# Moving the per-layer embedding's products behind the first experts, in a one-core decoder step

## The reference, cut to what matters

```
x = x + mixed @ w_o                                   # 520 rows of 1024
h2 = rmsnorm(x, g_ffn)
group: top 1 of 4; experts in it: top 2 of 8          # router, 36 logits per row
x = x + sum over the 2 chosen e of gate_e * (silu(h2 @ w_gate[e]) * (h2 @ w_up[e])) @ w_down[e]
gate = sigmoid(rmsnorm(x, g_ple) @ w_ple_gate)
x = x + (p @ w_ple) * gate                            # p: 520 rows of 256, an input
y = rmsnorm(x, g_final)
```

## Time and profile before

| | us |
|---|---|
| median of 3 runs | 1034.40 |
| the profiled execution | 1035.33 |
| its span in the trace | 1033.5 |
| TensorE busy | 867.0 (84%) |
| VectorE busy | 348.3 (34%) |
| ScalarE busy | 196.0 (19%) |
| GpSimd busy | 261.2 (25%) |
| DMA | 316.42 MB, mean 306 GB/s |
| chain that ended last | TensorE 53%, DMA 35% (the up weights 31%) |

### The profile page before, as it was taken

The page is one execution under the profiler, slowest core; times in us unless marked ns, Lnnn a source line. Parts: engine busy times, 40 slices in busy tenths (PEclk is TensorE's granted clock), DMA queues, the critical chain, the costliest instruction groups (busy, mean ns, idle before and its releaser), DMA issues.

```text
span 1033.5 us, 11650 instructions
## 1 busy us (share of the span) xinstructions
PE 867.0 (84%) x4281; PEld 450.8 (44%) x4281; DVE 348.3 (34%) x710; ACT 196.0 (19%) x393; POOL 261.2 (25%) x342
## 2 busy tenths in 40 slices
PE   5999888988969988899877878798877869783994
PEld 3888565755633545434332333233333323331442
DVE  5899966545424565213000000000000000011652
ACT  3110234423420121212101010101101011010431
POOL 6989775222210000202111110101111010001110
PEclk9999978998979996989998898988999898997998
DMA  9899954378994225269999999999999999997111
GB/s 308 325 337 381 326 211 164 133 280 346 361 370 166 101 103 212 73 256 414 404 408 400 408 403 407 413 395 412 410 408 420 394 410 403 428 408 295 74 42 41
DMA packets 53831, 316.42 MB, mean 306 GB/s; under 512 B 11246, under 2 KB 24110, under 8 KB 33048
## 3 DMA queue, kind: packets, MB, share of 16 engines
q1 hardware_dynamic: 34736, 233.28, 56.6%
q0 software_dynamic: 14480, 76.17, 19.4%
q10 hardware_dynamic: 4576, 6.46, 1.8%
HBM read 309.31 MB, written 14.82 MB: 314 GB/s over the span
## 4 chain that ended last, share of the span: by engine, by line
PE 53%; DMA 35%; DVE 5%; issue 2%; ACT 2%; POOL 2%; SPq 1%; POOLq 0%; DVEq 0%; ACTq 0%
DMA arena<-in_w_up 31%; PE psum L1692 14%; PE psum L1277 8%; PE psum L1359 7%; PE psum L1805 5%; PE psum L1507 5%; PE psum L1422 2%; PE psum L1644 2%; DMA arena<-in_w_down 1%; PE psum L1371 1%; DMA arena<-in_cache_v,indices 1%; PE psum L1401 1%; PE psum L1707 1%; PE psum L1530 1%; PE psum L1383 1%
## 5 line engine op out<-in xcount | busy, mean ns | idle before, releaser
L1692 PE MATMUL psum<-arena 128*64 128x512 f32 x1024 | 270.8, 689 | 82.3 <-DMA arena<-in_w_up 82.3
L1692 PEld LDWEIGHTS psum<-arena 128*64 128x64 f32 x1024 | 91.8, 158 | 237.3 <-issue 235.5
L2405 DVE TENSOR_TENSOR arena<-arena,psum 64x512 f32<-64x512 f32 x32 | 22.1, 691 | 376.2 <-ACT arena L1132 376.2
L1707 PE MATMUL psum<-arena 128*64 128x512 f32 x512 | 116.0, 592 | 3.6 <-DMA arena<-in_w_down 3.6
L1277 PE MATMUL psum<-arena 128*128 128x260 f32 x384 | 86.8, 388 | 0.1
L789 POOL COPY indices<-row_list 128x1 int32 (+1 forms) x26 | 4.6, 177 | 308.6 <-ACT arena L1138 308.6
L1359 PE MATMUL psum<-arena 128*128 128x260 f32 x320 | 80.1, 404 | 2.4 <-DVEq L1969 2.4
L1132 ACT ACTIVATE arena<-psum 64x512 f32<-64x512 f32 x32 | 18.9, 589 | 332.2 <-PE psum L1692 332.2
L720 POOL TENSOR_TENSOR arena<-arena 128x2048 f32<-128x2048 f32 x18 | 81.5, 4533 | 1.0 <-DMA arena<-in_cache_k,indices 0.7
L1277 PEld LDWEIGHTS psum<-arena 128*128 128x128 f32 x384 | 73.8, 193 | 12.8 <-issue 1.2
L1877 DVE TENSOR_REDUCE arena<-arena 128x32 f32<-128x2048 f32 x32 | 72.0, 2281 | 4.6 <-POOL arena L720 3.5
(11 more groups left out here) (331 smaller groups left out, 878.6 us busy)
## 6 DMA issues: line engine op xcount, KB each, us to landing
arena<-in_w_down SPq DMA_DIRECT2D x32, 2048.0 KB, 25.3
arena<-in_w_gate SPq DMA_DIRECT2D x31, 2048.0 KB, 18.4
arena<-in_w_up SPq DMA_DIRECT2D x31, 2048.0 KB, 22.9
arena<-in_w_in SPq DMA_DIRECT2D x11, 1024.0 KB, 7.6
arena<-in_x_prompt SPq DMA_DIRECT2D x8, 512.0 KB, 7.8
arena<-in_w_ple_gate SPq DMA_DIRECT2D x1, 4096.0 KB, 26.2
arena<-moe_rows SPq DMA_DIRECT2D x4, 1024.0 KB, 7.9
out<-arena ACTq DMA_DIRECT2D x8, 256.0 KB, 4.6
```

What stands on the lines that cost most here:

```text
L1692: last = mm(bank(s)[m * SLOTS:(m + 1) * SLOTS, :], hgT[s][:, k, :], w_gu[s][m][:, k, :], start=(k == 0), stop=(k == DC - 1))
L1707: last = mm(bank(6 + s)[n * SLOTS:(n + 1) * SLOTS, :], actT[s][:, k, :], w_dn[s][:, k, n * BANK:(n + 1) * BANK], start=(k == 0), stop=(k = ...
```

## The change

- The transposes of p (now transpose_p_tiles, three groups: tiles 0 and 4, tiles 1 and 2, tile 3) stand behind the experts 1, 2 and 3, and embed(0) to embed(4) behind the experts 4 to 8. They use banks 2 and 3, and wait for the counts and overflow lists that use the same banks.
- LEAD goes from RING + 1 = 5 to 2 * RING + 1 = 9: nine experts are written out on TensorE, VectorE and ScalarE, GpSimd's part likewise, and the loops begin a turn later.
- p's loads are issued by ScalarE behind the last stores of h2 instead of long before, to another place in SBUF; pT has one buffer per tile.
- The fills p01, p23 and p4 are gone, so the fills behind them change banks.
- On ScalarE copy_h2T(2) stands ahead of store_h2(QT). On VectorE second_norm(3) stands ahead of take_logits(QT).

```diff
-LEAD = RING + 1
+LEAD = 2 * RING + 1
+FIRST_LOOP = LEAD // RING
+P_MOVES = ((0, 4), (1, 2), (3,))
+EMBED_FROM = 1 + len(P_MOVES)
...
-         + ["rank1", "rank2"] + [f"h{QT}{s}" for s in "abr"] + ["p01", "p23", "p4"] + [f"h3{s}" for s in "abr"] + ["rank4", "rank3"])
+         + ["rank1", "rank2"] + [f"h{QT}{s}" for s in "abr"] + [f"h3{s}" for s in "abr"] + ["rank4", "rank3"])
...
-        pT = at(c4 + 2 * D, 2, NT)
-        p_nat = at(c4 + 2 * D + 2 * NT, TILES, DP)
+        p_nat = at(region_c + 3 * D, TILES, DP)
+        pT = [at(region_c + 3 * D + t * DP, 2, P) for t in range(TILES)]
...
 # ScalarE
             second_norm(QT)
+            copy_h2T(2)
             store_h2(QT)
-            copy_h2T(2)
             second_norm(3)
             copy_h2T(QT)
-            for name, t0, n in (("p01", 0, 2), ("p23", 2, 2), ("p4", 4, 1)):
-                wait_full(act, name)
...
             store_h2(3)
             copy_h2T(3)
...
-            copy_p_emb(0)
-            copy_p_emb(1)
             act.wait_ge(h2_stored[0], 48)
             act.wait_ge(h2_stored[1], 32)
-            for t in range(2, TILES):
-                copy_p_emb(t)
+            act.dma_start(p_nat[:, 0:QT, :], a["p_prompt"][0, 0].rearrange("(t p) n -> p t n", p=P)).then_inc(ple_in, 16)
+            act.dma_start(p_nat[0:NB, QT, :], a["p_sample"][0].rearrange("b l n -> (b l) n")).then_inc(ple_in, 16)
...
+                if 1 <= e < EMBED_FROM:
+                    copy_pT_tiles(e - 1)
+                if e >= EMBED_FROM:
+                    copy_p_emb(e - EMBED_FROM)
-            with act.Fori(1, NE // RING - 1) as i:
+            with act.Fori(FIRST_LOOP, NE // RING - 1) as i:
...
 # TensorE
             route(QT)
-
-            pe.wait_ge(ple_in, 48)
-            pes = (("p01", (0, 1)), ("p23", (2, 3)), ("p4", (4,)))
...
             transpose_h2(3)
-            embed(0)
             route_logits(3)
-            embed(1)
             rank_rows(QT)
             for t in (0, 1, 2):
                 list_rows(t)
-            embed(2)
             rank_rows(3)
             list_rows(QT)
             list_rows(3)
-            embed(3)
-            embed(4)
-
-            pe.wait_ge(pe_free, TILES)
...
+            def transpose_p_tiles(g):
+                if g == 0:
+                    pe.wait_ge(ple_in, 48)
+                if g == 1:
+                    pe.wait_ge(route_op, ROUTE_AT["over"])
+                if g == 2:
+                    pe.wait_ge(pe_free, 2)
+                for n, t in enumerate(P_MOVES[g]):
+                    w = tile_width(t)
+                    for k in range(2):
+                        first = n * 2 * P + k * P
+                        last = tr(bank(3 if g else 2)[:, first:first + w], p_nat[0:w, t, k * P:(k + 1) * P], ident[0:w, 0:w])
+                last.then_inc(pe_full, 1)
+
+            def embed(t):
+
+                w = tile_width(t)
+                pe.wait_ge(pe_free, len(P_MOVES) + t)
+                if t == 0:
+                    pe.wait_ge(lists_ready, 3)
+                for n in range(2):
+                    for k in range(2):
+                        last = mm(bank(2 + n)[0:w, :], pT[t][:, k, 0:w], w_ple_sb[:, k, n * BANK:(n + 1) * BANK],
+                                  start=(k == 0), stop=(k == 1))
+                last.then_inc(pe_full, 1)
...
             def list_over():
                 pe.wait_ge(route_op, ROUTE_AT["over"])
+                pe.wait_ge(pe_free, 1)
...
+                if 1 <= e < EMBED_FROM:
+                    transpose_p_tiles(e - 1)
+                if e >= EMBED_FROM:
+                    embed(e - EMBED_FROM)
-            with pe.Fori(1, NE // RING - 1) as i:
+            with pe.Fori(FIRST_LOOP, NE // RING - 1) as i:
...
 # VectorE
             place_rows(2)
+            second_norm(3)
             take_logits(QT)
-            second_norm(3)
             top_two(QT)
```

More of the change, by code:

```diff
@@ L192, in build @@
         assert c4 + 6 * D <= c3 + PAGE * HC
-        pT = at(c4 + 2 * D, 2, NT)
-        p_nat = at(c4 + 2 * D + 2 * NT, TILES, DP)
+        p_nat = at(region_c + 3 * D, TILES, DP)
+        pT = [at(region_c + 3 * D + t * DP, 2, P) for t in range(TILES)]
+        assert TILES * DP <= 2 * D
         w_gu = [[at(r + m * DC * BANK, DC, DE) for m in range(2)] for r in (region_b, region_a)]
@@ L375, in build @@
         lists_ready, list_full = sem("lists_ready"), sem("list_full")
-        ple_in, pe_full, pe_free = sem("ple_in"), sem("p_emb_full"), sem("p_emb_copied")
+        ple_in, pe_full, pe_free = sem("ple_in"), sem("p_full"), sem("p_copied")
         y_out = [sem(f"y_out{s}") for s in range(RING)]
@@ L812, in _ @@
             pool.wait_ge(lists_ready, 2)
-            for c in range(RING):
+            for c in range(FIRST_LOOP * RING):
                 move_rows(0, c)
             base = step.n
-            with pool.Fori(1, NE // RING - 1) as i:
-                step.off = (i - 1) * (2 * RING)
+            with pool.Fori(FIRST_LOOP, NE // RING - 1) as i:
+                step.off = (i - FIRST_LOOP) * (2 * RING)
                 for c in range(RING):
                     move_rows(i, c)
-            step.n, step.off = base + 2 * RING * (NE // RING - 2), 0
+            step.n, step.off = base + 2 * RING * (NE // RING - 1 - FIRST_LOOP), 0
             for e in range(NE - RING, NE + 2):
@@ L1044, in _ @@
             stored[0] += 4
-            act.wait_ge(rms_ready, 1)
-            act.dma_start(p_nat[:, 0:QT, :], a["p_prompt"][0, 0].rearrange("(t p) n -> p t n", p=P)).then_inc(ple_in, 16)
-            act.dma_start(p_nat[0:NB, QT, :], a["p_sample"][0].rearrange("b l n -> (b l) n")).then_inc(ple_in, 16)
             def second_norm(t):
@@ L1091, in _, with copy_pT_tiles @@
             second_norm(QT)
+            copy_h2T(2)
             store_h2(QT)
-            copy_h2T(2)
             second_norm(3)
             copy_h2T(QT)
-            for name, t0, n in (("p01", 0, 2), ("p23", 2, 2), ("p4", 4, 1)):
-                wait_full(act, name)
-                w = n * P if n == 2 else NB
-                act.activation(pT[:, :, t0 * P:t0 * P + w], fill(name).rearrange("p (k n) -> p k n", k=2)[:, :, 0:w],
-                               ACT.Copy).then_inc(free_of(name), 1)
             store_h2(3)
             copy_h2T(3)
+            act.wait_ge(h2_stored[0], 48)
+            act.wait_ge(h2_stored[1], 32)
+            act.dma_start(p_nat[:, 0:QT, :], a["p_prompt"][0, 0].rearrange("(t p) n -> p t n", p=P)).then_inc(ple_in, 16)
+            act.dma_start(p_nat[0:NB, QT, :], a["p_sample"][0].rearrange("b l n -> (b l) n")).then_inc(ple_in, 16)
+            def copy_pT_tiles(g):
+                act.wait_ge(pe_full, g + 1)
+                for n, t in enumerate(P_MOVES[g]):
+                    w = tile_width(t)
+                    src = bank(3 if g else 2)[:, n * 2 * P:(n + 1) * 2 * P].rearrange("p (k n) -> p k n", k=2)
+                    ins = act.activation(pT[t][:, :, 0:w], src[:, :, 0:w], ACT.Copy)
+                ins.then_inc(pe_free, 1)
             def copy_p_emb(t):
                 w = tile_width(t)
-                act.wait_ge(pe_full, t + 1)
-                pair = psum[0:w, 2 * (t % 2):2 * (t % 2) + 2, :]
-                act.activation(p_emb[0:w, t, :].rearrange("p (a n) -> p a n", a=2), pair, ACT.Copy).then_inc(pe_free, 1)
-            copy_p_emb(0)
-            copy_p_emb(1)
-            act.wait_ge(h2_stored[0], 48)
-            act.wait_ge(h2_stored[1], 32)
-            for t in range(2, TILES):
-                copy_p_emb(t)
+                act.wait_ge(pe_full, len(P_MOVES) + t + 1)
+                act.activation(p_emb[0:w, t, :].rearrange("p (a n) -> p a n", a=2), psum[0:w, 2:4, :], ACT.Copy).then_inc(pe_free, 1)
             def route_exps():
@@ L2416, in _ @@
                     overflow_lists()
-            with dve.Fori(1, NE // RING - 1) as i:
+            with dve.Fori(FIRST_LOOP, NE // RING - 1) as i:
                 for q in range(RING):
```

## The result

The kernel after took 1020.95 us, the median of 4 runs (1019.79 to 1022.33), against 1035.16 us for the kernel before (median of 4 runs, one more than the three behind 1034.40); the ratio is 0.9878, with a 95% interval of 0.9833 to 0.9922. Run again beside the experiments it gave 0.9908 (0.9878 to 0.9938) and 0.9855 (0.9830 to 0.9879). So the change makes the kernel 10 to 15 us faster. The forecast was 1019.3, a gain of 15.

What follows compares the result with a forecast made beforehand. The experts' weight stream bounds the kernel, its end set by expert 0's products. Savings 5.4 + 3.9 + 2.65 + 3.5 = 15.45 us take the profiled 1035.33 to 1019.9 and the median to 1018.95; forecast 1019.3, range 1015.5 to 1024.5.

Steps and rivals of the forecast that it cites:

- What bounds the kernel: Experts' weight stream, DMA busy from 447 to 930 us: the end follows when expert 0's gate and up products end.
- X: The date when SyncE issues expert 2's weights, at 446.30 us in the kernel before; the label comes from the experiments.
- Part A: Tile 2's copies ahead of the samples' store, up to T: 5.4 us earlier, 1.87 from waiting and 3.5 from clock.
- T: End of the last output projection half of tile 3, forecast to move from 398.71 to 393.35 us.
- Rival 1: TensorE's clock falls all the same at Part A's short gap, or another wait replaces it: price 3.5 us, time 1022.8, chance 0.15.
- Part B: T to R, with tile 3's norm first and p's work gone: 12.3 us in place of 16.2, 3.9 less.
- R: End of tile 3's router logits on TensorE, at 414.94 us in the kernel before.
- Part C: R to G, tile 3's placing no longer waiting for TensorE in embed(2): 8.4 us in place of 11.05, 2.65 less.
- G: Start of GpSimd's first gather, at 425.99 us in the kernel before.
- Part D: G to expert 0's products, without embed(3) and embed(4): 7.1 us in place of 10.6, 3.5 less.
- What is put behind: p's ten transposes and five embeds on TensorE behind experts 1 to 8: cost 0, covered by the weight queue's reserve.

Runs made afterwards that it cites:

- late_start: The kernel after with 16 idle TensorE products of 512 columns ahead of expert 0's gate and up products; 1032.14 us, ratio 0.9982 to the kernel before.
- no_swaps: The kernel after with both order swaps undone (tile 2's copies on ScalarE, tile 3's norm on VectorE), only p moved; 1024.80 us, ratio 0.9920 to before.
- no_embed: The kernel after without the five embeds' products, p_emb filled by ScalarE from a row of w_ple instead; 1021.26 us, ratio 0.9879 to before.
- double_embed: The kernel after with each embed's products issued twice, the second overwriting the first with the same values; 1023.57 us, ratio 0.9899 to before.
- lead_only: The kernel before with nine experts written out instead of five and loops from turn 2, nothing else; 1033.65 us, ratio 0.9999 to before.

## Why the prediction was right

Of the forecast 15.45 us, counted from the start of tile 2's transposes, the first profile after has 14.1 (64.13 to 50.04) and the two others 15.9 and 16.2.

- **What bounds the kernel**: right. X to the end is 587.2 before and after; with 14.3 us put ahead of X (late_start) it is 587.6.
- **Part A, up to T**: forecast 5.4, and the one part that came out otherwise in the recorded profile. The waiting was right: TensorE's gap is 0.89 us, forecast 0.95. The clock was right in five of eight profiles, which save 5.3, and wrong in three, the recorded one among them, which saves 3.6. Rival 1 (chance 0.15) named the cause, but at half its price: 1.7 us, not 3.5, because the clock stayed low about half as long (387.5 to 391.0, against 387.2 to 394.1 before). Its chance was set too low on a wrong reading: "after neither short one" overlooks the fall at 353 in the same trace, behind the short gap ahead of tile 0's logits. That the time still came within 1.7 us of the forecast owes something to that halved price.
- **Part B, T to R**: forecast 12.3, measured from the end of the projection half (396.30) to the end of tile 3's logits (408.54) 12.2. The logits at the low clock took 3.60, forecast 3.7. I had given 0.8 of it to the norm's swap; no_swaps shows 0.4: without the swap the samples' logits come 0.2 behind GpSimd's root and hold VectorE for 0.2, and then the norm starts.
- **Part C, R to G**: forecast 8.4, measured 416.96 - 408.54 = 8.4.
- **Part D, G to expert 0's products**: forecast 7.1, measured 424.04 - 416.96 = 7.1. The stored rows and p's loads were in nobody's way: the row transposes began at G + 4.1.
- **What is put behind**: cost 0 was right as far as the runs tell (no_embed), but the working had TensorE half a microsecond per expert behind the stream, with the queue to cover it and what the clock gives back left without a price. With the clock at 1.00 TensorE needed 15.7 against 16.1, so these five embeds did not draw on the queue; double_embed shows the queue at work. I expected TensorE's waits for up weights to shrink by nearly 20 us; they shrank by 15.3.
- **Written-out experts**: nothing that shows, as forecast (lead_only).

The median is 1.65 us above 1019.3, and the recorded profiled execution, 1022.33, is 2.4 above the 1019.9 forecast for one. In it two things fell short of the sum: 1.7 of the clock in A, and 1.16 by which tile 2's transposes began later than in the profile of before; 0.4 came back in expert 0's products (9.28 for 9.68). The second is no effect of the change: the same code ended that stage between 378.1 and 385.2 in thirteen profiles.

## What to carry to other kernels

Where a stream of loads is the bound, look for the date at which it can start and for what stands on the way to it; that work costs full price, and the same work behind the start costs nothing, up to the depth of the queue. Put a number on the depth (time from issue to landing less the transfer itself) and compare it with the lateness that the moved work adds up to, expert by expert: here five embeds fitted and ten did not. The estimate by issue and landing was 13 us; in double_embed 10.7 were absorbed. A wait taken away ahead of TensorE's work may be worth more than its length, because of the clock, but that part comes in some executions and not in others, so it belongs in the range rather than in the sum.

## What the runs showed of the hardware

- After the same gap of 0.89 us, ahead of tile 2's logits, TensorE's clock fell to the 1.2 GHz level in three profiles and stayed at 2.4 GHz in five. After 2.8 us it fell in all three. After an equally short gap ahead of tile 0's logits it fell in thirteen of thirteen, 1.7 to 4.7 us later and with TensorE busy.
- A float32 product of 512 columns written as one call is two instructions of about 0.43 us at full clock: 32 instructions for 16 calls, 16.51 us with part of them at the low clock.
- A store of 512 KB issued behind 6 MB of weights took 10.3 us to land (10.7 before), though it was on another engine's queue; a gather into quiet took 2.9.
